# Two chained transformer blocks in float32: four ring places of split weights moved by 32 bytes, a token sum by 64

## The reference

```python
def sqrelu_mlp(h, w1, w2):
    a = jax.nn.relu(h @ w1)
    return (a * a) @ w2

x = x + g1 * mixed
hx2 = modulate(rms_norm_2(x, norm2_g[l]), sh2, sc2)
x = x + g2 * sqrelu_mlp(hx2, w_mlp1[l], w_mlp2[l])
```

## Time and profile before

| what | us |
|---|---|
| median of 3 runs | 1579.6 (1579.44 to 1579.61) |
| the profiled execution | 1578.97 |
| its span, first to last instruction | 1577.2 |
| PE busy | 1559.1 |
| DVE busy | 1041.4 |
| ACT busy | 727.2 |
| the pairs of the last feed-forward, on PE | 1259.9 to 1397.3 |

### The profile page before, as it was taken

The page is one execution under the profiler, slowest core; times in us unless marked ns, Lnnn a source line. Parts: engine busy times, 40 slices in busy tenths (PEclk is TensorE's granted clock), DMA queues, the critical chain, the costliest instruction groups (busy, mean ns, idle before and its releaser), DMA issues.

```text
span 1577.2 us, 22557 instructions
## 1 busy us (share of the span) xinstructions
PE 1559.1 (99%) x8773; PEld 1310.3 (83%) x8773; DVE 1041.4 (66%) x1597; ACT 727.2 (46%) x1280; POOL 170.4 (11%) x191
## 2 busy tenths in 40 slices
PE   9999999999999999999999999999999999999998
PEld 7888878789887877788888788888888899998887
DVE  5688868956646677766534538666558898875554
ACT  5474456555234333343423445444444666643221
POOL 2012124501101000000000123421000000000000
PEclk9999999999999999999999999999999999999999
DMA  7365233211354896533324132222224143432222
GB/s 203 87 165 137 81 94 95 81 55 41 114 187 127 301 272 229 202 116 94 116 93 144 21 107 65 74 78 68 67 92 136 41 108 107 108 121 94 93 97 76
DMA packets 198581, 180.84 MB, mean 115 GB/s; under 512 B 6078, under 2 KB 178189, under 8 KB 195412
## 3 DMA queue, kind: packets, MB, share of 16 engines
q1 hardware_dynamic: 195056, 171.13, 35.5%
q10 hardware_dynamic: 2276, 6.95, 1.3%
q0 software_dynamic: 1152, 1.44, 0.6%
HBM read 175.15 MB, written 4.58 MB: 114 GB/s over the span
## 4 chain that ended last, share of the span: by engine, by line
PE 92%; DVE 4%; ACT 2%; issue 1%; DMA 0%; POOL 0%; ACTq 0%; DVEq 0%; POOLq 0%
PE acc L792 16%; PE acc L794 16%; PE acc L793 16%; PE acc L835 7%; PE acc L837 7%; PE acc L836 7%; PE acc L1340 2%; PE acc L850 2%; PE acc L1341 2%; PE acc L1342 2%; PE acc L848 2%; PE acc L849 2%; PE acc L1468 1%; PE acc L1484 1%; DVE w_low L2387 1%
## 5 line engine op out<-in xcount | busy, mean ns | idle before, releaser
L2387 DVE TENSOR_TENSOR w_low<-w_raw,w_high 128x1024 fp32r<-128x1024 f32 x202 | 251.2, 1245 | 363.9 <-ACT w_high L1603 363.4
L1603 ACT ACTIVATE w_high<-w_raw 128x1024 fp32r<-128x1024 f32 x194 | 205.7, 1060 | 498.5 <-PE acc L794 248.5
L792 PE MATMUL acc<-h_high,w_high 128*128 128x512 f32 (+1 forms) x976 | 384.6, 394 | 2.1 <-DVE h_low L2414 1.1
L794 PE MATMUL acc<-h_high,w_low 128*128 128x512 f32 (+1 forms) x976 | 377.1, 386 | 0.0
L793 PE MATMUL acc<-h_low,w_high 128*128 128x512 f32 (+1 forms) x976 | 376.6, 386 | 0.0
L792 PEld LDWEIGHTS acc<-h_high,w_high 128*128 128x128 f32 x976 | 183.4, 188 | 48.0 <-issue 9.6
L794 PEld LDWEIGHTS acc<-h_high,w_low 128*128 128x128 f32 x976 | 183.3, 188 | 37.7
L793 PEld LDWEIGHTS acc<-h_low,w_high 128*128 128x128 f32 x976 | 183.6, 188 | 36.0 <-issue 1.2
L835 PE MATMUL acc<-w_high,act_high 128*128 128x512 f32 x496 | 193.4, 390 | 0.9 <-DVE arena L2913 0.6
L836 PE MATMUL acc<-w_low,act_high 128*128 128x512 f32 x496 | 193.0, 389 | 0.0
L837 PE MATMUL acc<-w_high,act_low 128*128 128x512 f32 x496 | 193.0, 389 | 0.0
(11 more groups left out here) (461 smaller groups left out, 2694.0 us busy)
## 6 DMA issues: line engine op xcount, KB each, us to landing
w_raw<-w_in SPq DMA_DIRECT2D x68, 512.0 KB, 3.9
w_raw<-w_mlp SPq DMA_DIRECT2D x64, 512.0 KB, 4.0
w_raw<-w_up SPq DMA_DIRECT2D x44, 512.0 KB, 4.2
arena<-w_ada SPq DMA_DIRECT2D x13, 1024.0 KB, 8.3
w_raw<-w_out SPq DMA_DIRECT2D x24, 512.0 KB, 3.5
early<-w_ada SPq DMA_DIRECT2D x11, 1024.0 KB, 6.2
w_raw<-w_down SPq DMA_DIRECT2D x22, 512.0 KB, 3.4
w_raw<-w_branch_gate SPq DMA_DIRECT2D x16, 512.0 KB, 3.9
```

The lines of the kernel that those rows point to most:

```text
L792: pe.matmul(out_, wh, xh, start=start, stop=False, skip_group_check=skip)
L794: return pe.matmul(out_, wl, xh, start=False, stop=stop, skip_group_check=skip)
L1603: f(WH[:, off % 2, :], RAW[:, off % 4, :], ACT.Copy).then_inc(sem("w_high"), 1)
L2387: tt(WL[:, off % 2, :], RAW[:, off % 4, :], WH[:, off % 2, :].bitcast(F32), ALU.subtract).then_inc(sem("w_low"), 1)
```

## The change

`w_high` and `w_low` grow by 16 floats (64 bytes) in front. The two slots of all other stages begin behind these 16 floats, the ring's places 0 to 3 behind only 8 of them, so 32 bytes lower than the slots. Place 2 then begins 8 floats inside slot 0. The copy of the first gated rows into slot 0 therefore waits for one part more (part 94, which is the last in place 2). `token_sum` starts at 20456 floats of the arena instead of 20472. All buffers behind `w_low` move by 128 bytes.

In bytes modulo 128, from the old start of `w_high`: its slots go from 0 to 64, the slots of `w_low` stay at 0; places 0 to 3 go from 0 to 32 (high) and 96 (low); places 4 and 5 stay at 0; `token_sum` goes from 96 to 32; all other buffers stay.

```diff
-RAWT_, TOK_, SUM_ = M1_ + 20 * T, (20472, 23560, 25608), 27656
+RAWT_, TOK_, SUM_ = M1_ + 20 * T, (20456, 23560, 25608), 27656
...
-        WH = sb("w_high", [P, 2, 1024], F32R)
-        WL = sb("w_low", [P, 2, 1024], F32R)
+        WHW = sb("w_high", [P, 16 + 2048], F32R)
+        WLW = sb("w_low", [P, 16 + 2048], F32R)
+        WH, WL = (v[:, 16:2064].rearrange("p (a b) -> p a b", b=1024) for v in (WHW, WLW))
...
             at = (s + 4) % 6
             if at < 4:
-                c = slice(at % 2 * 512, at % 2 * 512 + 512)
-                return WH[:, at // 2, c], WL[:, at // 2, c]
+                c = slice(8 + at * 512, 8 + at * 512 + 512)
+                return WHW[:, c], WLW[:, c]
             return AH[:, at - 4, :], AL[:, at - 4, :]
...
                 if s == 7 * PAIRS - 3:
-                    gated_high(0, 7 * PAIRS - 4)
+                    gated_high(0, 7 * PAIRS - 3)
```

## The result

The changed kernel takes 1599.42 us (median of 4 runs, 1599.22 to 1599.65), against 1579.61 for the kernel before in the same comparison (1579.44 to 1579.78). The ratio is 1.0126, with a 95% interval of 1.0113 to 1.0138: 19.8 us slower. The forecast was 1579.4 with a range up to 1585.5.

A forecast was written before the change was run, and what follows sets the result against it. PE's matmul pace was taken to bound the pairs. The terms -0.2 + 0 + 0 + 0 + 0 gave -0.2 us on the median of 1579.6: 1579.4 us, range 1575.4 to 1585.5.

The forecast's parts named there:

- The bound: In the pairs nothing but the pace of PE's matmuls sets the time; PE never waits there.
- Part 1: Fourth part of each pair: moving the first token sum from 96 to 32 modulo 128 removes its excess, -0.2 us.
- Part 2: Ring places 0 to 3 in the pairs, 768 matmuls with moved weights: 0 taken, bounds -2.6 and +2.6 us.
- Rival B: In the pairs the relative start of weights and moving operand sets the pace: 1581.1 us, at worst 1582.0; chance 0.23.
- Part 3: Rest of the kernel: 3232 matmuls of 512 columns read w_high, now at 64 modulo 128; cost taken as 0.
- D: Rival: w_high at 64 modulo 128 slows 512-column matmuls of the whole kernel; 1583.3 us, 1590.1 with the full step; chance 0.20.
- the full step: On the 3232 matmuls reading w_high: 3.3 ns each, taken from 256-column rows (120.0 against 116.7), 10.7 us.
- Parts 4 and 5: End gated copy waits one part more, cost 0 (at most 0.6 us uncovered); ACT and DVE splits at moved places, cost 0.

The follow-up runs named there:

- Experiment 4: The kernel before with 64 unused bytes ahead of w_high, so every buffer moves by 64 bytes and the distances stay: 1579.35 us, ratio 0.9999.
- experiment 6: The kernel before with token_sum alone moved, to 20424 floats (32 modulo 256): 1579.09 us, ratio 0.9998.
- experiment 1: The kernel before with token_sum alone moved, to 20456 floats (96 to 32 modulo 128): 1579.69 us, ratio 1.0003.
- experiment 5: The kernel before with the w_high and w_low slots moved by 256 bytes, ring places 0 to 3 at 160 (high) and 224 (low) modulo 256: 1580.16 us.
- experiment 7: The kernel before with the slots of w_high and w_low both at 64 modulo 256 from all other buffers: 1600.05 us, ratio 1.0130.

## Why the prediction was wrong

**The bound.** That PE's pace alone sets the time was right, in the pairs and elsewhere: 19.4 of the 20.2 us of span are busy time of PE. One wait of PE grew, that for the low part of h ahead of the first block's feed-forward, from 0.2 to 1.6 us; it is where the kernel before ran at half the clock (504 to 508 us) and the changed one did not, so PE was ready sooner and waited instead. Experiment 4 has the same longer wait and the time of before, so this is no part of the loss.

**Part 1, the token sum: wrong in its sign alone, right in its cause.** "The low rows of token_sum differ from token_sums in nothing but where they read" holds: moved by 48 x 4 = 192 bytes to 32 modulo 256 the excess is gone (experiment 6). But the step read the places modulo 128, in which 20456 floats is the good place. In experiment 1 it made the fourth part 1.44 us, 0.3 us more in all where 0.2 less was forecast. In the changed kernel, where the weights of four places have moved too, it takes 1.41 on average.

**Part 2, the ring: 0 was taken, 0.7 us came.** The bounds of 2.6 to either side held. The reason given for the 0 ("where the moving operand starts, which this part leaves alone") is refuted by experiments 4 and 5: if every buffer moves, nothing happens, and if only the ring's weights move, the pairs grow from 137.41 to 138.17 us. So it was always the distance. Rival B had that idea with the wrong modulus: by it the high weights at the same 32 as the moving operand would have paid like a distance of 0, while modulo 256 they are 128 apart.

**Part 3, the rest of the kernel: the step that failed.** "Modulo 64 nothing moved for them. I take 0." The term came out at 19.9 us. Read start to start over all matmuls of a kind, less the waits of PE, it is 6.0 us on the 2832 products with h (2.1 ns each), 11.2 on the 1488 down products (7.5 each) and 2.7 on the 384 of lines 1340 to 1342 (7.1 each). The pairs add 0.7 and the smaller groups with these weights 0.2. PE's waits ahead of all these are 0.5 shorter, which leaves 20.3 of the 20.4 us by which the last matmul starts later.

The mechanism was among the rivals, as D, with 0.20. It was right that the 512-column matmuls of the whole kernel pay. Its price was too low: it took 1.2 ns from the token sum, and 3.3 ns from the 256-column rows for the full step. Its count was too low as well: 3232 has only the matmuls that read w_high, and a third of the loss, 7.3 of the 19.9 us, lies in steps of the 1568 others, which read w_low and whose own distance did not change (5.4 of it in line 836). A step runs to the start of the next matmul, so a part of this may belong to the neighbour; counted by the step ahead of it, line 836 still has 4.2 us.

A row of the right size was there. The earlier trace rows shows 512 columns at 226.7 and at 233.1 ns: 6.4 ns x 3232 = 20.7 us, 1600.3. The prediction used these two rows to show that the order turns round, and then priced a change in 512-column matmuls with the 256-column step. Had D been priced from its own width, the range would have had to reach 1600. That this figure falls so near the measured 1599.4 is luck: some 4700 matmuls paid 4.2 ns on average, not 3232 of them 6.4.

The table does not explain all of the loss. The down products take 234.4 ns where the moving operands alternate between 192 (w_high) and 0 (w_low) from the weights, while both at 192 cost 233.3 and both at 0 cost 226.7. Two in three at 192 and one at 0 would be 231.1. By such sums the three kinds of products would have lost some 12 us, not 19.9. The steps of lines 835, 836 and 837 in the changed kernel are 235.4, 237.7 and 230.0 ns, so the slowest one starts with a matmul whose own distance is 0. The next matmul's weights are loaded while it runs: this load starts together with the second of the seven down products shown above.

```profile
1452.00 0.19 PEld L838 LDWEIGHTS acc<-w_high,act_low 128*128 128x128 f32 x1
```

But those weights, in act_low, are at distance 0 from w_low too, so the place of the next weights does not account for this step. What differs from the uniform runs is that one moving operand follows another at a different place. No run separates that, and the cause of this part of the loss, some 7 us, stays open.

The Trainium skill ("TensorE: Matmul & The Clock Gate", Step-by-step: what each phase is for) says that loading the next weights takes no read bandwidth from the running matmul. By that rule the place of the weights could not matter. Here it does: in experiment 7 the weights of h alone moved, and the pace went from 226.8 to 233.3 ns. The measurement decides. Whether read bandwidth is what is lost, no run shows.

**Parts 4 and 5: right.** The gated copy waited 0.52 us, was done 0.84 us ahead of DVE's use, and cost nothing. PE waited for no split in the pairs.

**The chances.** Slower by over 0.2% had 0.21. The evidence was read as 64 bytes being nearly neutral because one row (the token sum at 96 instead of 32 modulo 128) cost only 1.2 ns. That row compared 224 with 32 modulo 256, two places of a curve that goes up and down (the table), at the other width. It said nothing on the places that the change came to.

## What to carry to other kernels

In a kernel whose matmuls run without a gap, the distance between the stationary and the moving operand's start is a tuned quantity: a pad in front of one buffer moves it for every user of that buffer. Pad by what keeps all distances (here a shift of everything, experiment 4, or 256 bytes on the weights, experiment 5), or give the special stage a view inside the buffer and leave the rest where it is. And when an edit shifts a buffer that the whole kernel reads, price it from rows of the width and kind of those matmuls, times their count, even if the argument says zero.

## What the runs showed of the hardware that was not expected

- The period is neither 64 nor 128 bytes: 128 bytes on w_high cost 20 us, 256 bytes nothing. All of this fits a period of 256.
- The sign counts: a distance of 64 gives 228.9 ns, 192 gives 233.3, at 512 columns.
- The best distance depends on the width: 0 for 512 columns (226.7 ns; every other one in the table costs 2.2 to 7.6 ns), 16 or 32 bytes for 256 columns (116.7; at 0 it is 120.0, the worst). In the second case 98 parts in a row took 1.400 us each, to the resolution of the trace.
- At 256 columns 8 bytes are like 0 (120.0 ns), 16 like 32 (116.7), 48 between (118.3). At 512 columns 8 bytes are not like 0 (233.3 against 226.7).
- A mix of distances can be slower than each of them: 234.4 ns where 192 and 0 alternate (233.3 and 226.7 by themselves). Why is open.
- Distances such as 24, 80 or 112 bytes were not tried. What makes the period, and why parts at 160 bytes differ, no run shows.
